# RWKV triangular inverse: the level mask moves from GpSimd, ahead of the product, to VectorE, behind it

## The reference

```
def step(S, inp):
    r_t, w_t, k_t, v_t, kk_t, a_t = inp
    sa = einsum('bhvk,bhk->bhv', S, kk_t)
    S = S * w_t[:, :, None, :] - sa[..., None] * (kk_t * a_t)[:, :, None, :] + v_t[..., None] * k_t[:, :, None, :]
    return S, einsum('bhvk,bhk->bhv', S, r_t)
s_fin, y = lax.scan(step, s0, xs_t)          # token by token
```

## Time and profile before

| what | value |
|---|---|
| timed runs, median (lowest to highest) | 3595.38 us (3587.19 to 3597.66) |
| the profiled execution's own time | 3574.97 us |
| its span, first to last instruction | 3573.2 us |
| PE busy, PEld busy | 2946.2 us (82%), 2633.9 us (74%) |
| DVE, ACT, POOL busy | 1443.5 us (40%), 853.6 us (24%), 331.4 us (9%) |
| mean granted TensorE clock (1 is 2.4 GHz) | 0.909 |
| L1175 (masked copies on POOL) | 45 instructions, median 1092 ns |
| L821 (copies of the product on ACT) | 45 instructions, median 585 ns |

### The profile page before, as it was taken

One profiled execution on the slowest core, in us unless ns is written; L12 is line 12 of the kernel. 1 busy time (PEld: TensorE's weight loads), 2 busy tenths in 40 slices (PEclk: granted clock), 3 DMA queues, 4 the chain that ended last, 5 costly groups with the idle time before them and its releaser, 6 DMA issues. The chain is left out here.

```text
span 3573.2 us, 55249 instructions
## 1 busy us (share of the span) xinstructions
PE 2946.2 (82%) x23634; PEld 2633.9 (74%) x23634; DVE 1443.5 (40%) x1979; ACT 853.6 (24%) x1528; POOL 331.4 (9%) x251
## 2 busy tenths in 40 slices
PE   2997888884888879894699999999143999999993
PEld 2997777763555556662599999999123999999993
DVE  4143555534343434305533333333777333333335
ACT  2112444312333334202211111111222111111111
POOL 0222344310000013101000000000100000000001
PEclk9997999956898989897799999999576999999996
DMA  2110000001000036320111111110050111111111
GB/s 85 47 41 16 3 3 3 3 14 52 1 7 9 0 118 213 107 97 0 41 42 47 41 46 42 47 41 29 4 20 30 42 47 41 47 41 47 41 41 50
DMA packets 53487, 147.06 MB, mean 41 GB/s; under 512 B 21840, under 2 KB 22224, under 8 KB 52592
## 3 DMA queue, kind: packets, MB, share of 16 engines
q1 hardware_dynamic: 44144, 107.45, 10.6%
q0 software_dynamic: 9216, 37.75, 3.1%
HBM read 137.67 MB, written 7.51 MB: 41 GB/s over the span
## 5 line engine op out<-in xcount | busy, mean ns | idle before, releaser
L393 PE MATMUL ps<-h_ffn,mlp_split 128*128 128x362 f32 (+1 forms) x4608 | 769.4, 329 | 64.9 <-DVE mlp_split L562 64.9
L393 PEld LDWEIGHTS ps<-h_ffn,mlp_split 128*128 128x128 f32 x4608 | 766.9, 190 | 67.0 <-issue 67.0
L393 PE MATMUL ps<-mlp_u,mlp_split 128*128 128x362 f32 (+1 forms) x4608 | 768.1, 328 | 11.0 <-DVE mlp_u L574 11.0
L393 PEld LDWEIGHTS ps<-mlp_u,mlp_split 128*128 128x128 f32 x4608 | 761.2, 189 | 15.7 <-DVE mlp_u L574 15.7
L580 DVE TENSOR_TENSOR y<-y,ps 128x362 f32<-128x362 f32 (+1 forms) x384 | 181.4, 528 | 466.5 <-PE ps L393 466.5
L533 ACT CAST mlp_split<-mlp_raw 128x1024 fp32r<-128x1024 f32 x128 | 134.3, 1049 | 619.6 <-PE ps L393 608.0
L572 DVE TENSOR_TENSOR mlp_relu<-mlp_relu 128x1088 f32<-128x1088 f32 x64 | 82.7, 1293 | 489.5 <-ACT mlp_relu L546 489.5
L393 PE MATMUL ps<-h,in_split 128*128 128x362 f32 (+1 forms) x1440 | 242.5, 331 | 33.6 <-POOL in_split L454 33.6
L393 PEld LDWEIGHTS ps<-h,in_split 128*128 128x128 f32 x1440 | 242.2, 190 | 34.7 <-issue 34.7
L246 POOL TENSOR_TENSOR x<-x,y 128x1088 f32<-128x1088 f32 x12 | 41.7, 3474 | 2048.4 <-DVE y L301 2048.4
L546 ACT ACTIVATE mlp_relu<-ps 128x362 f32<-128x362 f32 (+1 forms) x192 | 77.0, 475 | 532.0 <-PE ps L393 532.0
(11 more groups left out here) (385 smaller groups left out, 3651.2 us busy)
## 6 DMA issues: line engine op xcount, KB each, us to landing
mlp_raw<-w_mlp_dram SPq DMA_DIRECT2D x128, 512.0 KB, 3.6
in_raw<-w_in_dram SPq DMA_DIRECT2D x20, 512.0 KB, 3.5
x<-x_dram SPq DMA_DIRECT2D x2, 4352.0 KB, 14.7
y_dram<-x SPq DMA_DIRECT2D x1, 4352.0 KB, 11.7
out_ring<-w_out_dram SPq DMA_DIRECT2D x8, 512.0 KB, 3.6
pa_w<-w_pair_dram SPq DMA_DIRECT2D x4, 640.0 KB, 4.0
pa_rope<-rope_dram SPq DMA_DIRECT2D x1, 1088.0 KB, 6.7
ckv_dram<-z SPq DMA_DIRECT2D x1, 1088.0 KB, 8.9
```

What stands on the lines that cost most here:

```text
L393: last = self.nc.tensor.matmul(out, w[:, a, k, m], rhs[:, b, rk, at:at + c], start=(start and n == 0), stop=(stop and n == 2))
```

## The change

The mask constant is transposed (`level_T` becomes `levels`). `level_p` on TensorE now multiplies with the unmasked half of `MB`. The product in PSUM bank 2 is read by VectorE, multiplied by the mask and written to `PM` (`masked_level`, the first instruction of VectorE's `level`). ScalarE's five copies of a block and GpSimd's five masked copies go. TensorE issues the same matmuls in the same order, and only the wait on `level_b` goes.

```diff
-                  ("pair_ident", HD), ("grams", P), ("grams_s", P), ("below", HD), ("below_T", HD), ("level_T", LEVELS * HD),
+                  ("pair_ident", HD), ("grams", P), ("grams_s", P), ("below", HD), ("below_T", HD), ("levels", LEVELS * HD),
...
-    put("level_T", np.concatenate([(row // (2 << n) == col // (2 << n)) & (col >> n & 1 == 1) & (row >> n & 1 == 0)
+    put("levels", np.concatenate([(row // (2 << n) == col // (2 << n)) & (row >> n & 1 == 1) & (col >> n & 1 == 0)
                                    for n in range(1, LEVELS + 1)], 1))
...
-                    def level(j, n):
-                        w = slice(0, width(j))
-                        wait("prod_p", j, n)
-                        nc.scalar.copy(PM[w, :, :, :], ps[w, 2, :].rearrange("p (e a k) -> p e a k", e=2, a=PAIRS)).then_inc(g["p_out"].sem, 1)
-
...
-                            level(B, 1)
...
-                        if has(B):
-                            level(B, 5)
...
+                    def masked_level(j, n):
+
+                        w = slice(0, width(j))
+                        mask = self.c("levels", w, lo=HD * (n - 1), hi=HD * n).unsqueeze(1).to_broadcast([width(j), H, HD])
+                        wait("prod_p", j, n)
+                        tt(PM[w, :, :, :].rearrange("p e a k -> p (e a) k"), bank(2, H, HD)[w], mask, ALU.mult).then_inc(g["p_out"].sem, 1)
+
                     def level(j, n):
                         w = slice(0, width(j))
 
...
+                        masked_level(j, n)
                         wait("prod_x", j, n)
...
-                    def level_b(j, n):
-                        w = slice(0, width(j))
-                        wait("mb_out", j)
-                        wait("prod_p", j - 1, n)
-                        mask = self.c("level_T", w, lo=HD * (n - 1), hi=HD * n).unsqueeze(1).unsqueeze(1).to_broadcast([width(j), 2, PAIRS, HD])
-                        tt(BT[n - 1][w, :, :, :], MB[j % 2][w, :, :, 0, :], mask, ALU.mult).then_inc(g["level_b"].sem, 1)
-
...
-                        if has(B):
-                            level_b(B, 1)
-                            level_b(B, 2)
...
-                        if has(B):
-                            level_b(B, 3)
...
-                        if has(B):
-                            level_b(B, 4)
-                            level_b(B, 5)
...
                     def level_p(j, n):
-                        wait("level_b", j, n)
                         if n == 1:
                             wait("x0", j)
...
-                                end = mm(ps[c, 2, HD * (PAIRS * e + p):HD * (PAIRS * e + p) + HD], BT[n - 1][c, e, p, :], X[c, e, p, :], start=True, stop=True)
+                                end = mm(ps[c, 2, HD * (PAIRS * e + p):HD * (PAIRS * e + p) + HD], MB[j % 2][c, e, p, 0, :], X[c, e, p, :], start=True, stop=True)
```

More of the change, by code:

```diff
@@ L637, in rwkv @@
                  "key_back", "kk_done", "cumulated", "exps", "ke_in", "ab_in", "rk_in", "bonus_sum", "bonus_v", "bonus_done", "kp_in",
-                 "kr_in", "bp_in", "turned_v", "turned_k", "turned_b", "turned_kk", "v_out", "k_out", "b_out", "kk_out", "gram_mb", "mb_out", "gram_mk", "mk_out", "gram_a", "x0", "level_b",
+                 "kr_in", "bp_in", "turned_v", "turned_k", "turned_b", "turned_kk", "v_out", "k_out", "b_out", "kk_out", "gram_mb", "mb_out", "gram_mk", "mk_out", "gram_a", "x0",
                  "prod_mv", "mv_out", "prod_p", "p_out", "prod_x", "x_out", "prod_wg", "wg_out", "prod_r", "y_in", "rhat",
@@ L642, in rwkv @@
         g = {n: self.counter(n) for n in names}
-        per_block = {"mb_out": 2, "mk_out": 2, "level_b": LEVELS, "prod_p": LEVELS, "p_out": LEVELS,
+        per_block = {"mb_out": 2, "mk_out": 2, "prod_p": LEVELS, "p_out": LEVELS,
                      "prod_x": LEVELS, "x_out": LEVELS, "step": 2, "state": 2, "y_in": 2, "rhat": 2, "f_out": 2, "tt_out": 2}
@@ L883, in _ @@
                                 nc.scalar.copy(Fs[p % 2][:, :, :], bank(4 * (p % 2) + 1, DB, HD)).then_inc(g["s_fout"].sem, 1)
-                        if has(B):
-                            level(B, 2)
                         if has(C):
                             square(C)
-                        if has(B):
-                            level(B, 3)
                         if has(A):
@@ L895, in _ @@
                             gn_root(C)
-                        if has(B):
-                            level(B, 4)
                         if has(A):
                             b_out(A)
-                        if has(B):
-                            level(B, 5)
                         if has(K) and K:
```

## The result

The changed kernel takes 3619.9 us (median of 8 runs, 3613.72 to 3639.32), the kernel before 3596.52 (8 runs, 3587.19 to 3600.57). By the medians it is slower by 23.4 us, where 25.8 were forecast. The ratio of the means is 1.0079, which is 28.5 us, with a 95% interval from 1.0057 to 1.0101. The profiled execution took 3619.62 us.

What follows compares the result with a forecast made beforehand. TensorE was taken to set the pace, through the chain of inverse levels. Six iterations (19.6 us), blocks 7 and 8 (5.0) and block 0 (1.2) add 25.8 us to the timed median 3595.38: 3621 us, range 3604 to 3641.

Steps and rivals of the forecast that it cites:

- signs: Level_x waits about 2.2 us (level 1) and 1.4 (level 5), removed_key 0.7 each, earlier table load, no lora wait, period near 48.2.
- Level 1: The masked evacuation stands behind block C's second state step on VectorE, so level_x starts late: +2.30 us an iteration.
- Level 2: The evacuation stands behind removed_key, no longer held by GpSimd, so level_x starts slightly late: +0.24 us an iteration.
- Rival 2: At level 2 GpSimd and removed_key still meet, costing 2.2 us instead of 0.24; 3633 us, chance 0.07.
- Levels 3 and 4: TensorE's own fillers between level_p and level_x cover the new evacuation: 0 us.
- Level 5: Evacuation behind key(K) delays level_x by 1.56 us; lora's earlier start returns part, leaving +0.72 us an iteration.
- The price of a hand-over: From the end of a VectorE instruction to the TensorE matmul waiting for it: 0.15 us.
- the removed wait: Beyond lora's 0.76 us, no TensorE wait for ScalarE's or GpSimd's copies was left to remove: nothing gained.
- Ends of the stage: Blocks 7 and 8 get 2.5 us each and block 0 about 1.2, outside the six full iterations.
- The sum: 3.26 us an iteration, 19.6 over six; with the end blocks 25.8 us, giving a median of 3621 us.
- rival 1: New gaps, above all at level 1, make TensorE's clock fall: 18 us more, 3639 us, chance 0.11.
- Rivals 3 and 4: Relief of GpSimd wins, 3579 us, chance 0.03; waits at levels 4 and 5 absorb the delay, 3595, chance 0.05.

Runs made afterwards that it cites:

- e_level1: Changed kernel with level 1's masked evacuation issued behind the first state step, ahead of kept_key(A) and the second state step; 3601.00 us, one run.
- e_pool2: Changed kernel with GpSimd's five masked copies per block put back, their output read by nobody; 3624.56 us, one run.
- e_level5: Changed kernel with level 5's masked evacuation issued ahead of key(K) instead of behind it; 3612.85 us, one run.
- e_sig: Kernel before with ScalarE's sigmoid step and its table load moved ahead of the level-5 copy; 3597.78 us, one run.
- e_wait: Changed kernel with one more, long-fulfilled wait (on mb_out) ahead of each level_p; 3623.81 us, one run.
- e_best: Changed kernel with the masks of levels 1, 2 and 5 all issued earlier on VectorE; 3595.83 us (12 runs), ratio 1.0003 to the kernel before.
- e_sig5: Kernel before with ScalarE's sigmoid step ahead of its level-5 copy, repeated and timed; 3592.78 us against 3591.49, ratio 1.0003.

## Why the prediction was right, and which terms were off

The mechanism was as forecast, and its signs came: waits of 2.11 and 1.38 us at levels 1 and 5, `removed_key` at 0.69, the table load ahead of level 5, no wait of `lora`. The period came out at 47.5 and not 48.2.

*Level 1, forecast 2.30.* Measured 2.27 (4.93 - 2.66). e_level1 shows that it is VectorE's order.

*Level 2, forecast 0.24.* Measured 0.25 (2.41 - 2.16), with `removed_key` at 0.69 as forecast. Rival 2 didn't come; e_pool2 shows what it would have cost in the changed order, 0.92.

*Levels 3 and 4, forecast 0.* Measured -0.01 and 0.00.

*Level 5, forecast 0.72.* Measured 0.63: 1.46 at `level_x` (forecast 1.56, less by the shorter hand-over), and 0.83 back from `lora` (forecast 0.84). e_level5 and e_sig show the two halves apart. `weigh` cost nothing, as counted.

*The term that was mis-sized.* The price of a hand-over was taken as 0.15 everywhere, and the removed wait at nothing ("no wait of TensorE for them is left to remove"). That held for the waiting, not for the wait itself: without it each of five `level_p` in an iteration starts 0.1 us sooner, 0.47 in all (3.57 to 3.47, 3.56 to 3.46, and so on, between `level_x` and the next `level_p`). So 2.27 + 0.25 - 0.01 + 0.63 - 0.47 = 2.67, the measured iteration, where the forecast had 3.26. Of the 0.59 between them the removed wait is 0.27, as e_wait shows. The other 0.32 is the hand-over from the mask to `level_x` at levels 1, 2 and 5, each 0.05 (513.82 to 513.87 at level 1) where the forecast had 0.15. That level 1 came out as close as 2.27 hides this: its `level_p` starts 0.1 sooner and its `level_x`, which waits for VectorE, does not; in e_wait it is 2.18 (4.84 - 2.66).

*Ends of the stage.* Block 0 got 1.5 us more of TensorE's idle time (forecast 1.2), block 7 2.2 to 2.4 and block 8 1.4 to 2.1 (forecast 2.5 each).

*The sum.* TensorE's idle time in the stage grew by 19.8 us in the first pair of profiles and by 19.9 in the second, where the forecast had 25.8 (14.7 and 13.9 in the six iterations, forecast 19.6). The prediction took all six at 44.87, but blocks 5 and 6 of the kernel before have a late fall both times. Another 10.3 to 12.1 us are the same matmuls, busy longer: the stage grew by 30.1 and 32.0. This part is rival 1, which came in part. Of it, 7.0 and 8.0 us lie in the three iterations of six that have the early fall at the wait of level 1 (block 6 has a longer late fall as well); the prediction had priced one such fall at 2.2 in every block. Blocks 7 and 8 together have 4.7 and 3.6 more (75.60 and 78.91 busy, against 70.88 and 75.30), and the second level of the last block runs at the lower clock after the change and not before. TensorE of the changed kernel there, where the second level's product takes 1.97 (725.67 with 1.11 in the kernel before, shown above):

```profile
752.86 1.97 PE L1347 MATMUL ps<-rw_X,rw_MB 64*64 64x64 f32 x16
```

The timed difference of 23.4 (28.5 by the means) lies between 19.8 and 30.1, with an interval of 20.5 to 36. So the forecast of 25.8 was near it by two errors of opposite sign, which is luck: the idle time was put 6 too high, and the sum had the clock's part at nothing. How large the clock's part is in the timed runs is not shown: e_wait, in the order of the changed kernel, had no early fall and was busy no longer (342.4) than the kernel before in its second profile (342.3). Why the clock falls one level sooner in the last block stays open, too. It does so in every run with level 1's mask behind the state step and not in e_level1 and e_best, but also in e_sig and e_sig5, which have no such mask.

*Rivals 3 and 4* fell: the undisturbed iteration did not get shorter, and the waits at levels 4 and 5 ahead of `level_p` are there as before (1.39 and 1.39 against 1.48).

## What to carry to other kernels

Ask of moved work not which engine is idle, but what stands ahead of it in the order of the engine that gets it: 1.75 us more busy time on VectorE gave TensorE 3.66 us of new waits an iteration (2.11, 0.17 and 1.38), because three masks stood behind instructions that had time; issued ahead of them, they cost nothing that could be measured. Compare profiles by iterations at full clock and by idle time of the engine that sets the pace; that repeated to 0.2 us here, while whole spans of the same kernel lay 26 us apart. And where a clock falls, look for the place inside the iteration: the count of fallen iterations hid here that the costly falls all stood behind one new wait.

## What the hardware showed that I had not expected

- A matmul that waits for VectorE starts 0.05 us after it in the changed kernel, and 0.15 where a long-fulfilled wait stands ahead of that one (e_wait, and the kernel before). A fulfilled wait behind it cost nothing (level 1's `level_x`, 513.82 to 513.87).
- GpSimd holds an instruction of VectorE with both inputs in SBUF until about the end of its own (0.69 to 1.60 us in e_pool2, to 1.33 in e_level1), also a short one: the state step takes 0.82 at 512.39 in the changed kernel, where GpSimd is at work, and 0.41 to 0.42 where it is not. Instructions with an input in PSUM kept their 0.68 to 0.69.
- TensorE's granted clock dropped to the 1.2 GHz level right at a wait of 2.1 us in 15 of 30 iterations, and at that place in none of 42 with a wait of 0.81 or none. Which of the waits have a fall differs between two runs of one kernel.
